# Whole pieces of the gates' projection in the steps of the stick phase

## The reference

```
h = rmsnorm(x, g);  z = h @ w_in        # q, k, v and gates of A, B, C, and 3 x 1024 merge gates gm
# branch B: stick-breaking attention, 8 heads of 64; prompt: keys 0..2047, sample: 4096 cached keys + 16
s = q @ k.T * d**-0.5
log_rest = where(causal, log_sigmoid(-s), 0)
A = where(causal, exp(log_sigmoid(s) + suffix_sum(log_rest)), 0);  ob = A @ v
merged = sigmoid(gm[0]) * ya + sigmoid(gm[1]) * yb + sigmoid(gm[2]) * yc
y = rmsnorm(x + merged @ w_out, g_final)
```

## Time and profile before

| what | value |
|---|---|
| median of 3 runs | 3130.05 us (3121.77 to 3133.41) |
| profiled execution | 3126.34 us |
| its span, first to last instruction | 3124.7 us |
| mean granted TensorE clock | 0.971 |
| TensorE busy | 2913.1 us, 93% of the span |
| VectorE busy | 1508.2 us, 48% |
| GpSimd busy | 1139.2 us, 36% |
| ScalarE busy | 1004.7 us, 32% |
| DMA | 485.98 MB, mean 156 GB/s |

### The profile page before, as it was taken

One profiled execution on the slowest core, in us unless ns is written; L12 is line 12 of the kernel. 1 busy time (PEld: TensorE's weight loads), 2 busy tenths in 40 slices (PEclk: granted clock), 3 DMA queues, 4 the chain that ended last, 5 costly groups with the idle time before them and its releaser, 6 DMA issues. The chain is left out here.

```text
span 3124.7 us, 50524 instructions
## 1 busy us (share of the span) xinstructions
PE 2913.1 (93%) x20331; PEld 2384.2 (76%) x20331; DVE 1508.2 (48%) x2135; ACT 1004.7 (32%) x1843; POOL 1139.2 (36%) x1001
## 2 busy tenths in 40 slices
PE   6899999999987999989998999799997996999798
PEld 5788888888876888767765777577776776877686
DVE  7332221000004667557765676567767784433333
ACT  6441111111112444334433444344435562000221
POOL 4332331111113445445544455344545563333100
PEclk9999999999998999999999999999998998999899
DMA  6543332212235544664556555755447347444443
GB/s 213 176 156 116 129 122 73 71 69 73 70 97 174 166 150 161 215 204 158 173 190 226 184 164 173 235 179 174 149 160 217 115 149 227 165 162 168 168 141 108
DMA packets 383016, 485.98 MB, mean 156 GB/s; under 512 B 27889, under 2 KB 241905, under 8 KB 382417
## 3 DMA queue, kind: packets, MB, share of 16 engines
q1 hardware_dynamic: 341200, 359.32, 36.5%
q0 software_dynamic: 34688, 111.05, 9.5%
q10 hardware_dynamic: 6912, 12.59, 1.2%
HBM read 359.28 MB, written 123.60 MB: 155 GB/s over the span
## 5 line engine op out<-in xcount | busy, mean ns | idle before, releaser
L376 PE MATMUL prj_bank<-hidden_hi,w_hi 128*128 128x512 f32 (+2 forms) x1360 | 491.4, 361 | 12.9 <-DVE w_lo L439 12.9
L378 PE MATMUL prj_bank<-hidden_hi,w_lo 128*128 128x512 f32 (+2 forms) x1360 | 487.6, 359 | 0.0
L377 PE MATMUL prj_bank<-hidden_lo,w_hi 128*128 128x512 f32 (+2 forms) x1360 | 487.2, 358 | 0.0
L1103 POOL TENSOR_TENSOR stk_beta<-stk_beta,stk_left 128x1024 f32<-128x1024 f32 (+4 forms) x160 | 275.8, 1724 | 574.2 <-DVE stk_left L1020 574.2
L812 PE MATMUL stk_g_bank<-hidden_hi,w_hi 128*128 128x512 f32 (+2 forms) x928 | 378.1, 407 | 28.2 <-ACT stk_g_out L940 17.4
L814 PE MATMUL stk_g_bank<-hidden_hi,w_lo 128*128 128x512 f32 (+2 forms) x928 | 340.6, 367 | 0.0
L813 PE MATMUL stk_g_bank<-hidden_lo,w_hi 128*128 128x512 f32 (+2 forms) x928 | 339.2, 366 | 0.0
L966 ACT ACTIVATE stk_beta<-stk_z 128x1024 f32<-128x1024 f32 (+2 forms) x224 | 180.9, 807 | 389.3 <-PE stk_z L857 191.9
L1067 DVE COPY stk_a_t<-stk_turn_bank 128x512 f32<-128x512 f32 (+4 forms) x456 | 230.5, 546 | 156.1 <-PE stk_turn_bank L884 154.5
L376 PEld LDWEIGHTS prj_bank<-hidden_hi,w_hi 128*128 128x128 f32 x1360 | 257.1, 189 | 44.3 <-DVE w_lo L439 13.1
L378 PEld LDWEIGHTS prj_bank<-hidden_hi,w_lo 128*128 128x128 f32 x1360 | 256.9, 189 | 32.4
(11 more groups left out here) (254 smaller groups left out, 5366.7 us busy)
## 6 DMA issues: line engine op xcount, KB each, us to landing
stk_kd<-in_cache_sb_k SPq DMA_DIRECT2D x64, 1024.0 KB, 6.2
stk_vd<-in_cache_sb_v SPq DMA_DIRECT2D x64, 1024.0 KB, 7.3
w_raw<-in_w_in SPq DMA_DIRECT2D x112, 512.0 KB, 3.9
scratch_zT<-stk_g_out POOLq DMA_DIRECT2D x72, 256.0 KB, 2.3
mrg_gate<-scratch_zT SPq DMA_DIRECT2D x24, 768.0 KB, 4.4
scratch_zT<-prj_z POOLq DMA_DIRECT2D x48, 256.0 KB, 2.3
prj_w<-in_w_in SPq DMA_DIRECT2D x18, 512.0 KB, 3.9
mrg_u_raw<-scratch_uT SPq DMA_DIRECT2D x9, 1024.0 KB, 9.1
```

The costliest lines, as they stand in the source:

```text
L376: pe.matmul(out, w_hi[u][:, k, :], hi[:, k, :], start=k == 0, stop=False)
L377: pe.matmul(out, w_hi[u][:, k, :], lo[:, k, :], start=False, stop=False)
L378: last = pe.matmul(out, w_lo[u][:, k, :], hi[:, k, :], start=False, stop=k == KC - 1)
L1103: pool.tensor_tensor(bt, bt, left[prompts.index(n) % 2][:, :, 1:keys + 1], ALU.mult).then_inc(a_done, 1)
```

## The change

Two edits. In `shares` a step takes the whole current piece or nothing. It takes it when the allowance saved up reaches 0.9 of the piece's cost, and in a step that turns keys (`s + 1 in kblocks`) when it reaches 0.25 of it. In `gates_part` the piece is cut in two halves of four slices only in a step that turns keys; elsewhere all eight slices stand in the second place, behind the turning of A.

```diff
-        out, p, k, have, pause = [], LEAD, 0, 0.0, 0
+        out, p, have, pause = [], LEAD, 0.0, 0
         for s in range(N + LAG_O):
             have += weight[s] * per
-            first = k
-            if p == GN or pause:
+            ahead = KC * cost[p] * (0.25 if s + 1 in kblocks else 0.9) if p < GN else 0
+            if p == GN or pause or have < ahead:
                 pause = max(0, pause - 1)
                 out.append(None)
                 continue
-            while k < KC and have >= cost[p] / 2:
-                have -= cost[p]
-                k += 1
-            out.append((p, first, k) if k > first else None)
-            if k == KC:
-                pause = 5 if p in turn_over else 0
-                p, k = p + 1, 0
-        return out, [(q, k if q == p else 0, KC) for q in range(p, GN)]
+            have -= KC * cost[p]
+            out.append((p, 0, KC))
+            pause = 5 if p in turn_over else 0
+            p += 1
+        return out, [(q, 0, KC) for q in range(p, GN)]
@@ gates_part
-                    mid = (k0 + k1) // 2
+                    mid = (k0 + k1) // 2 if s + 1 in kblocks else k0
```

## The result

The changed kernel takes 3094.40 us (median of 4 runs, 3091.68 to 3096.85) against 3126.39 us of the kernel before in the same comparison: ratio 0.9901, 95% interval 0.9884 to 0.9919. The forecast of 3116 (3098 to 3134) was wrong: the direction was right, but the gain is 32.0 us where 14 were forecast. Of the 21.6 us between 3116 and 3094.4, 3.7 are the base: the forecast started from a median of 3130.05, and with one more run it is 3126.39. The other 18 us are the change's. The profiled execution took 3091.68 us, its span 3090.0 against 3124.7 us.

What follows compares the result with a forecast made beforehand. TensorE was taken as the bound in the long stretches. Terms -6.4 - 15.0 - 4.8 + 10.5 made -15.7 us, less 1.8 dropped: 3126.3 - 13.9 = 3112.4, or 3116 with the runs' median 3.7 us higher; range 3098 to 3134.

Steps and rivals of the forecast that it cites:

- (a): Five key-turning steps lose their gates, so the next scores wait for copies: 1.0 us each, 5 us added.
- Blocks of gates: 142 gate blocks leave the place between output products and turning of A, each giving back 0.045 us: -6.4 us.
- Waits that go: TensorE's waits for the gate bank, key copies and cache values end, 13.5 us, plus 1.5 us of clock: -15.0 us.
- Loads of keys: Key turnings at steps 114 and 172 wait less for their DMA, by 1.5 and 3.3 us: -4.8 us.
- Added: New costs on TensorE from steps without gates and from the last pieces: +10.5 us.
- (b): In runs of steps without gates, output products wait for the bank VectorE takes over: 0.16 us for each of 32, 5 us.
- (c): The last pieces run in steps 234 and 236, behind the last chain: 0.5 us added.
- The clock: Clock dips behind waits at steps 10, 16 and 62, up to 1.7 us each; one counted, 1.5 us.
- more than counted: Rival: clock dips go, pauses begin with full queues, (b) stays at 0: -21 to -40 us, 3090 to 3109, chance 0.18.
- Waits come back: Rival: only the blocks' 6.4 us and a few waits stay, (a) and (b) eat the rest: 3119 to 3131, chance 0.20.
- VectorE takes over: Rival: output products wait for the bank in runs of steps without gates: up to 47 us, 3143 to 3158, chance 0.09.

Runs made afterwards that it cites:

- e2: The kernel before with its old table, but the gates of a step that turns no keys stand whole behind the turning of A: 3111.93 us, ratio 0.9957.
- e3: The kernel before with the gate slices of steps 10, 16 and 59 moved to the next step: 3123.28 us, ratio 1.0001.
- e8: The kernel before with only its first six steps changed: whole pieces at steps 1, 3 and 5, no gates at 0, 2 and 4: 3118.20 us, ratio 0.9981.
- g1: The kernel before with the loads of the keys of steps 114 and 172 asked for first, at steps 112 and 170: 3114.97 us, ratio 0.9970.
- e7: The changed kernel with gates put back at its five key-turning steps that had none: 3094.53 us, ratio 0.9910 to the kernel before.
- e5: The changed kernel with SyncE asked for keys ahead of weights and the next round's keys and queries: 3151.56 us, ratio 1.0077 to the kernel before.

## Why the prediction was wrong

Most of the forecast's mechanisms are in the runs. What failed are two steps of the sum: the list of waits began at 985 us and so put the waits of steps 0 to 4 at nothing, and the load of keys at step 114 was taken at 1.5 of 5.7 us. The added term (a) was also too large. By the forecast's own parts:

- **Blocks of gates, -6.4 us: the mechanism right, the price a little low.** e2 takes 6.6 us out of steps 21 to 58 and the three plain stretches, where little else can change. These hold 106 of the blocks (141 in all by the table of shares, not 142), so a block gives back 0.062 us, not 0.045, and the match of 6.6 with 6.4 is partly luck. The trace of before says the same when all of its blocks are read instead of one: between the output products and the turning a block costs 0.12 to 0.13 us beyond 0.227 us for each matmul (medians), and the turning behind gates is 0.06 us shorter (four transposes 0.35 us against 0.41, eight 0.79 against 0.85). A block behind the turning costs 0.19 to 0.21 us in the same way, but without it the turning is 0.17 us longer up to the next scores (four transposes 0.59 us against 0.41 in the trace of after). So making gates rarer pays almost nothing, and keeping them out of the place between the output products and the turning pays.
- **Waits that go, -15.0 us: the places right, the worth not shown.** The gate bank waits of 5.3 us are gone. The waits of 3.3 us in the turnings of steps 7, 25 and 65 are gone too, but one of 1.8 us has come in step 11, so that together these waits fell by 1.7 us (5.6 and 1.0 to 4.9) between 985 and 1360 us. Those for values of the cache fell by 2.1 of 2.3 and 1.4 of 2.6 us. But e3, which removes three of the gate bank waits alone, gives less than 2.8 us. That they paid in the changed kernel because the chains beside them got shorter too is my reading, and no run shows it.
- **The start, not counted.** This is the largest single miss. I began my list of waits at 985 us, and the ones of 6.8 and 3.9 us lay in the stretch ahead. The steps up to 20 got 14.9 us shorter in the profiles, 10 to 11 with like first waits; the forecast had 3.9 + 0.9 us of waits, 1.5 us of clock and under 1 us of blocks there, 7 us. e8 gives 6.6 us for the spacing of the first pieces alone, and e2 has 4.9 us of its gain in the same steps.
- **Loads of keys, -4.8 us: the term that was mis-sized.** It was worth 9.2 us (g1). At step 172 I had taken the whole wait, and it went. At step 114 I had expected 3 to 5 us of it to remain, and nothing did. I took 1.5 of 5.7 us there, "with VectorE and GpSimd less behind", because the piece ahead ends in the same step in both tables. What counted was the distance in time: in the changed kernel the weights and the loads of the next round left SyncE 1.1 us before the buffer was free, in the one before 3.2 us after it. The row of SyncE at 1616.43 us would have shown what stood ahead of the load at step 114, as the earlier trace rows did for 172. The dips of the clock behind both waits, some 3 us by the forecast's own price of up to 1.7 us each, had no term.
- **Added, +10.5 us.** (a) 5 us for gateless turnings: too much. The scores behind each of the five turnings wait 0.44 us, 2.2 us in all, where I took 1.0 each, and e7 gives nothing back in all and 0.6 and 0.7 us at two of them. The row of 2.45 us in the earlier trace rows was misread: it stands wholly at the lower clock (0.50 from 1355.0 to 1358.4 us), not partly. At the full clock such scores take 1.31 us, as those of step 114 behind the turning of step 113:

```profile
1600.78 1.31 PE L867 MATMUL stk_z<-stk_kd_t,stk_qd 128*32 128x512 f32 x8 [0.44 <-DVE stk_kd_t L1056]
```

- Of the same term, (b) 5 us for the output bank: right, 5.6 us more of such waits in the trace. From e2 to the changed kernel the three plain stretches get 1.8, 3.0 and 2.7 us longer, and these waits are most of it. They use up the gain of the blocks there, hence the zeros in the table above. The mark that I had set, "if the phase is over 25 us shorter, (a) and (b) were hidden", was wrong for (b). (c) 0.5 us: too small to tell.
- **The clock.** I counted one dip of three, 1.5 us. From step 0 on, the time at the lower clock fell from 68.3 to 47.8 us. All three of my dips are gone (1010.2 to 1013.6, 1047.8 to 1051.2, 1314.0 to 1317.4 us) and so are the two behind the late keys (from 1628.0 and 1972.8 us). Of the 35 us, 20 are waits: TensorE's from step 0 on sum to 70.4 us before and 50.4 after. The other 15 are the lower clock and the work itself; each instruction's excess over its usual spacing gives 6 to 8 us for the clock, a rough figure. One sentence of the prediction was also wrong of the trace of before: it had the clock fall behind all waits of 2 us and more. It fell behind the one of 1.7 us in step 16, and stayed at 1.00 behind the one of 2.6 us in step 178 (2004.86).

Put together: the missing start (6.6 us by e8), 4.4 us more for keys, 2.8 us of (a), and 6 us that the place brought beyond the term for blocks (e2's 12.4 less 6.4, most of it in the start, its cause open) are 19.8 us; the smaller rows of the second point lose some 3 of them. 14 + 17 is near the 32 measured. Each of these terms has an interval of 3 us or more, so the agreement says no more than that nothing large is missing. Of the rivals, "more than counted" (chance 0.18, 3090 to 3109 us) is what came in the number. Of its three reasons one is right (the clock dips go). The pauses did not get shorter (26.7 and 26.8 us for the first, 29.7 and 29.5 for steps 123 to 127), and (b) did not stay at 0. Its range held the result mainly through the start and the keys, which it did not name. "Waits come back" is what e3 does, and "VectorE takes over" never came near: the largest wait for the bank is 1.0 us.

## What to carry to other kernels

Before summing up a schedule change, list the waits of the whole phase, its first steps included, and compare only between points at which both orders have done the same work: the gain then shows in a few places, and long stretches at the bound give nothing. Before reading a stretch of one trace as a gain, see how much it differs between two runs with the same instructions: here the start did by 4 to 7 us. A load that is late on a shared in-order queue was worth about its wait here (9.2 us for waits of 9.0), but asking for it first makes others late: check what then stands behind the request, on that queue and on the engine that takes the next load. A wait that is removed alone may pay next to nothing (e3), since the chain beside it may be nearly as late.

## What the runs showed of the hardware

- One load of 1 MB of keys took 5.6 us from issue to landing when asked for ahead of the others (g1: 1614.7 to 1620.3), 9.4 us behind one of weights and four of keys and queries that had left 1.6 to 3.6 us earlier (the changed kernel), and 12.3 us right behind them (before). In these three cases the order on the queue made more difference than the moment of the issue.
- A matmul of 512 columns behind products of another kind holds TensorE for 0.314 us; the next three positions have 0.229 to 0.233 us, and from the seventh on it is 0.227 us (medians of the spacing in the traces of before and after, at the full clock). The cost of changing over is paid once in a run.
- In the changed kernel a wait of 0.77 us (1471.83) left the granted clock at 1.00 in the windows from 1470 to 1482 us. In e5 a wait of 1.31 us ended at 1479.40 and one of 1.62 us at 1482.21; during the second the granted clock fell to 0.50, that is 1.2 GHz, and it stayed there from 1481.2 to 1488.0 us. In the kernel before it fell behind a wait of 1.71 us (1047.66) and not behind one of 2.59 us (2004.86): the length of a wait alone doesn't tell.
